# Two requests at a time on TensorE's column tiles for page scores and dilated values, and memory values with the weights as the stationary operand

## The chip, the cores and the metric

The kernel runs on one core of one Trainium2 chip. Its time is the device time of one launch in microseconds (us). Three runs of the kernel before gave 2172.45, 2179.99 and 2188.25 us, a median of 2179.99 us. A further run was recorded by the hardware profiler; every row below is from that one.

## The reference, cut to what matters

One decoder layer for two groups that share the weights: a prompt of 1024 tokens and 8 requests ("samples") of 4 new tokens each, with 1024 past keys. Everything is float32. Three small pieces of the samples' work matter here.

```python
# index scores of a request's 4 tokens against its 1024 past keys (pages of 128) and its new ones, 8 index heads
dots = einsum('bqhd,bsd->bqhs', qi, ki)                     # b = 8 requests, d = 64
score = einsum('bqh,bqhs->bqs', wi * IDX_SCALE, relu(dots)) # then the 256 best keys per token

# dilated windows, 3 groups with (window, dilation) = (128,1), (512,4), (2048,16), 4 heads of 64
kv_sel = kv_all[:, lb + t - dil * arange(m + 1)]            # per request
p = softmax(einsum('bqhd,bqkhd->bqhk', q, kv_sel[..., 0]) * scale)
o = einsum('bqhk,bqkhd->bqhd', p, kv_sel[..., 1])           # <- values, per request

# memory attention, 256 memory tokens per request, 4 heads of 64
p = softmax(einsum('bqhd,bkhd->bhqk', q, mem_kv[:, :, 0]) * scale)
o = einsum('bhqk,bkhd->bqhd', p, mem_kv[:, :, 1])           # <- values, per request
```

## The kernel before, in words

The program is a row of stages, each a block in which the five engines run their own instruction lists and meet by semaphores.

**Stage 1 (`project_and_select`, about 0 to 717 us)** projects all 1056 tokens with `w_in`, in 138 steps of 24 float32 products split in three (high and low halves of both operands). Steps 0 to 89 put tokens on the output's partitions (L955), steps 90 to 137 compute the gates (L961; nine steps for each 384 columns). Between two steps TensorE does pieces of other work, by a table of steps:

- `PAGES_AT`: steps 44, 46, ..., 60. At step 44 + 2b, `turn_pages(b)` transposes the index keys of request b (8 transposes, L1019) into `pt`; ScalarE's `take_pages(b)` copies them to `kis_t[:, b % 2]`; and `dot_pages(b - 1)` scores the request before (L1028: 64 rows of contraction, a stationary operand of 32 columns, two halves of 512 moving columns). Request b's 32 rows (4 tokens by 8 heads) are partitions `32 * (b % 4)` on of `big[:, b // 4]`.
- VectorE picks the best keys in rounds (`best`: MAX8 L859, MATCH_REPLACE8 L862). In its last 24 rounds it also sums one "window unit" a round (L893, `s_logit`).
- A window unit is one (group, request) of `WIN_UNITS`, 24 in all, group by group. SyncE loads queries and keys (`load_near`, from step 86 on; the query load of unit u waits for logit u - 3), GpSimd multiplies (`products`, L762 to L767), VectorE sums. At step 127 (`LOGITS_AT`) TensorE turns the logits (L1071), and SyncE starts loading values.
- `READ_AT`: after each of the steps 131 to 136, `read_values` of four units in turn. Group 0 has one matmul a unit, groups 1 and 2 have four (one for each residue t). All have a stationary operand of 32 columns (`spread[g]`, where the weights of a pair of requests stand side by side in zeros) and 256 moving columns of values (L1091), and add to 32 partitions of `big[:, 1, 0:256]`: `row = 32 * (b // 2)`. So the two requests of a pair share a row strip. The values of unit u are in `v_near[u % 4]`; the load of unit u waits for the read of unit u - 4 (`s_read`), at L444. A unit's values are 128 KB in group 0, 512 KB in group 1, 256 KB in group 2 (64 partitions).

**Stage 4 (paged attention of the samples)** is not changed, but it does similar work: `score_pair` (L2087) issues the matmuls of two requests one behind the other into different strips of 32 partitions, and its values (L2131) go over four strips in turn.

**Stage 6 (`attend_mem`, about 1295 to 1450 us)** does the memory attention. The samples' part lies inside the prompt's: in iteration `it` TensorE computes logits of prompt tile `it` (L2853), transposes the weights of tile `it - 1` (L2873, after ScalarE's four exponentials, L2615), and multiplies tile `it - 2` with the values (L2885). At `it == 0` it turns the samples' weights (L2801); at `it == 1` it runs `mem_values` (L2810): for each request, each half c of the 256 value columns and each half a of the memory tokens, one matmul with the values as the 128 x 128 stationary operand and the request's 16 columns of weights as the moving one. The result is already transposed, and ScalarE's `sample_rows` (L2599) and VectorE's `sample_low` (L2711) take it out of `p_o`. The values of prompt tile 0 at `it == 2` reuse `p_o`, so TensorE waits for `sample_low` (`s_slo`).

In the profile one float32 matmul appears as two MATMUL records. The line numbers are those of the profile.

Of the kernel before, what the change touches and what calls it, by code (L numbers as in the profile page):

```python
# [91 lines left out]
WIN_UNITS = [(g, b) for g in range(3) for b in range(DB)]  # L92
# [82 lines left out]
def project_and_select(nc, d, sel, spare):  # L175
# [6 lines left out]
    with ctx:  # L182
# [204 lines left out]
        with nc.Block() as block:  # L387
# [541 lines left out]
            def _(pe):  # L929
# [92 lines left out]
                def dot_pages(b):  # L1022
                    u, r = b // 4, 32 * (b % 4)
                    pe.wait_ge(s_kptev, b + 1)
                    if b == 0:
                        pe.wait_ge(s_relu, len(dots))
                    for e in range(2):
                        m = pe.matmul(big[r:r + 32, u, 512 * e:512 * e + 512], qis_t[:, u, r:r + 32], kis_t[:, b % 2, 512 * e:512 * e + 512],  # L1028
                                      start=True, stop=True)
                    m.then_inc(s_sdot, 1)  # L1030
# [50 lines left out]
                def read_values(u):  # L1081
                    g, b = WIN_UNITS[u]
                    w = WIN_KEYS[g]
                    row = 32 * (b // 2)
                    if u == 0:
                        pe.wait_ge(s_ptev, 1)
                        pe.matmul(big[:, 1, 0:256], probs_new, v_new, start=True, stop=False, skip_group_check=True)
                    pe.wait_ge(s_vnear[u % 4], 16 * (u // 4 + 1))
                    for t in range(WIN_RES[g]):
                        x = 32 * (b * WIN_RES[g] + t)  # L1090
                        m = pe.matmul(big[row:row + 32, 1, 0:256], spread[g][0:w, x:x + 32], v_near[u % 4][0:w, t * 256:(t + 1) * 256],  # L1091
                                      start=False, stop=True, skip_group_check=True)
                    m.then_inc(s_read, 1)

                for s in range(FIRST_STEP[NIDX], len(STEPS)):
# [7 lines left out]
                    if s in PAGES_AT:  # L1103
                        b = PAGES_AT[s]
                        if b < DB:
                            turn_pages(b)
                        if b:
                            dot_pages(b - 1)
# [12 lines left out]
                    for u in READ_AT.get(s, []):  # L1121
# [1320 lines left out]
def attend_mem(nc, d, km_t, vm, h_t, n, inv_in, inv_out, w_first, w_first_r, gains, kept):  # L2442
# [6 lines left out]
    with ctx:  # L2449
# [20 lines left out]
        probs_st = sb("probs_st7", [P, 2, P])  # L2470
# [30 lines left out]
        s_sptev = sem("f_sptev")  # L2501
        s_spv = sem("f_spv")
# [36 lines left out]
        with nc.Block() as block:  # L2539
# [20 lines left out]
            def _(act):  # L2560
# [29 lines left out]
                def sample_weights():  # L2590
                    act.wait_ge(s_spt, 1)
                    act.activation(probs_st[:, :, :], p_x[:, 0:256].rearrange("p (a c) -> p a c", a=2), ACT.Copy).then_inc(s_sptev, 1)
# [9 lines left out]
                for it in range(LAST):  # L2602
# [15 lines left out]
                    if it == 1:  # L2618
                        sample_weights()
                    if it == 2:  # L2620
# [26 lines left out]
            def _(pool):  # L2647
                pool.memset(q_bd[:, :, :], 0.0).then_inc(s_pad, 1)
# [1084 lines left out]
```

## Time and profile before

| | |
|---|---|
| median of three runs | 2179.99 us |
| the profiled run's own time | 2187.04 us |
| its span (first to last instruction) | 2185.3 us |
| TensorE matmul busy | 2027.0 us (93%) |
| VectorE, ScalarE, GpSimd busy | 1282.0, 718.0, 579.9 us |
| mean granted TensorE clock | 0.956 |

### The profile page before, as it was taken

Reading aid. Unit: us, or ns where it says so; the run is one execution under the profiler, and the core shown is the slowest. Engines: PE = TensorE matmul, PEld = TensorE weight load, DVE = VectorE, ACT = ScalarE, POOL = GpSimd, SP = SyncE. Lnnn points to the kernel's source line nnn. Section 1 sums busy time; section 2 is a strip of 40 time slices with the busy share of each in tenths; the row PEclk is TensorE's granted clock in tenths of the full one; section 3 lists DMA queues with packets and bytes.
Section 4 is the critical chain, followed back from the end, with each engine's and each line's share of the span. In section 5 each row is a group of like instructions: output and inputs, shape, how many; then the busy total and the mean of one; then the engine's idle time right before and its main releaser. Section 6 shows DMA issues by size and latency. Waiting matters only on the chain. (4 is left out here: it accounts for less than half of the span.)

```text
span 2185.3 us, 35149 instructions
## 1 busy us (share of the span) xinstructions
PE 2027.0 (93%) x13531; PEld 1850.8 (85%) x13531; DVE 1282.0 (59%) x2470; ACT 718.0 (33%) x1478; POOL 579.9 (27%) x671
## 2 busy tenths in 40 slices
PE   6999899999999786889779989999999999999997
PEld 6878788999996675555469989899999999999997
DVE  5049999998770342554337323677676676653535
ACT  5233222112220554334322124563233233332523
POOL 5786646678970001100100120120000000301000
PEclk9999999999999887799889998899999999999999
DMA  5022132346744613784336202012222222534434
GB/s 177 15 86 77 64 93 69 103 154 196 238 150 149 230 55 85 239 282 157 98 117 203 68 20 89 10 56 69 84 81 72 84 80 73 197 120 153 135 90 138
DMA packets 227162, 254.16 MB, mean 116 GB/s; under 512 B 51684, under 2 KB 209540, under 8 KB 226484
## 3 DMA queue, kind: packets, MB, share of 16 engines
q1 hardware_dynamic: 192292, 170.92, 25.9%
q0 software_dynamic: 8080, 51.13, 6.5%
q10 hardware_dynamic: 26624, 29.87, 3.9%
q8 instruction: 108, 1.77, 0.3%
q14 instruction: 58, 0.48, 0.1%
HBM read 205.18 MB, written 74.00 MB: 128 GB/s over the span
## 5 line engine op out<-in xcount | busy, mean ns | idle before, releaser
L955 PE MATMUL pz<-w_hi,n_hi 128*128 128x384 f32 (+2 forms) x720 | 246.5, 342 | 1.7 <-ACT z L537 1.0
L955 PE MATMUL pz<-w_hi,n_lo 128*128 128x384 f32 (+2 forms) x720 | 240.5, 334 | 0.0
L955 PE MATMUL pz<-w_lo,n_hi 128*128 128x384 f32 (+2 forms) x720 | 240.5, 334 | 0.0
L862 DVE MATCH_REPLACE8 sel<-m,sel 128x1024 f32<-128x1024 f32 (+4 forms) x224 | 205.4, 922 | 0.0
L859 DVE MAX8 m<-sel 128x8 f32<-128x1024 f32 (+4 forms) x224 | 197.6, 926 | 0.2
L3575 PE MATMUL p_c<-n_t_hi,blk 128*128 128x264 f32 x1120 | 191.3, 285 | 1.8 <-DVE blk L3292 1.8
L3575 PEld LDWEIGHTS p_c<-n_t_hi,blk 128*128 128x128 f32 x1120 | 159.0, 188 | 2.0 <-issue 2.0
L955 PEld LDWEIGHTS pz<-w_hi,n_hi 128*128 128x128 f32 x720 | 138.8, 193 | 24.5 <-issue 21.3
L3575 PE MATMUL p_c<-mix_hi,blk 128*128 128x264 f32 x816 | 141.1, 285 | 0.0
L955 PEld LDWEIGHTS pz<-w_lo,n_hi 128*128 128x128 f32 x720 | 138.9, 193 | 0.0
L955 PEld LDWEIGHTS pz<-w_hi,n_lo 128*128 128x128 f32 x720 | 138.8, 193 | 0.0
L961 PE MATMUL pz<-n_hi,w_hi 128*128 128x352 f32 x384 | 125.7, 327 | 3.5 <-ACT z L531 3.5
L537 ACT ACTIVATE z<-pz 128x384 f32<-128x384 f32 (+2 forms) x90 | 42.7, 475 | 251.7 <-PE pz L955 211.3
L961 PE MATMUL pz<-n_lo,w_hi 128*128 128x352 f32 x384 | 124.1, 323 | 0.0
L961 PE MATMUL pz<-n_hi,w_lo 128*128 128x352 f32 x384 | 124.1, 323 | 0.0
L3575 PEld LDWEIGHTS p_c<-mix_hi,blk 128*128 128x128 f32 x816 | 116.4, 189 | 0.0
L727 POOL TENSOR_TENSOR rot<-z,rope 128x384 f32<-128x384 f32 (+3 forms) x90 | 75.6, 840 | 152.9 <-ACT z L537 150.9
L709 POOL TENSOR_TENSOR w_lo<-w_raw,w_hi 128x1536 fp32r<-128x1536 f32 (+3 forms) x32 | 106.1, 3315 | 36.0 <-ACT w_hi L504 36.0
L3575 PE MATMUL p_c<-n_t_lo,blk 128*128 128x264 f32 x560 | 113.9, 284 | 0.0
L3175 POOL DMA_DIRECT2D g_s<-gate x22 | 12.0, 545 | 368.6 <-DVE gate L3380 343.5
L1302 DVE CUSTOM_DVE_ANT_0 probs<-p_s,masks 128x128 f32<-128x128 f32 (+1 forms) x96 | 28.1, 349 | 137.1 <-PE p_s L1367 130.8
L3616 PE MATMUL p_c<-n_t_hi,blk 128*128 128x264 f32 x540 | 105.0, 286 | 1.6 <-DVE blk L3406 0.9
(485 smaller groups left out, 5265.6 us busy)
## 6 DMA issues: line engine op xcount, KB each, us to landing
w_raw<-in_w_in SPq DMA_DIRECT2D x26, 768.0 KB, 4.8
blk_raw<-in_w_ffn_in SPq DMA_DIRECT2D x72, 256.0 KB, 2.9
relu<-z_qb SPq DMA_DIRECT2D x24, 512.0 KB, 4.8
blk_raw<-in_w_ffn_out SPq DMA_DIRECT2D x58, 192.0 KB, 2.5
z_b<-z ACTq DMA_DIRECT2D x48, 192.0 KB, 1.9
gates<-z ACTq DMA_DIRECT2D x48, 176.0 KB, 3.1
gate<-gates SPq DMA_DIRECT2D x24, 352.0 KB, 3.4
out_new_win_sample<-in_cache_win_kv POOLq DMA_DIRECT2D x8, 1016.0 KB
```

Source lines behind the costliest of these rows:

```text
L537: act.activation(z[:, u, 0:w], pz[:, s % 2, 0:w], ACT.Copy).then_inc(s_zev, 1)
L709: pool.tensor_tensor(w_lo[:, n % 2, 4 * j:4 * j + 4, 0:w], w_raw[:, f % RAW, :, 0:w], w_hi[:, n % 2, 4 * j:4 * j + 4, 0:w].bitcast(F32), A ...
L727: pool.tensor_tensor(a, z[:, u, 0:nh * HD].rearrange("p (h e) -> p h e", h=nh), cos, ALU.mult)
L859: dve.max(out=m8[0:r, u, :], in_=sel[0:r, o:o + n]).then_inc(s_max, 1)
L862: dve.match_replace(out=sel[0:r, o:o + n], in_to_replace=m8[0:r, u, :], in_values=sel[0:r, o:o + n], imm_value=PICKED).then_inc(s_rep, 1)
L955: m = pe.matmul(out, tokens(a, k, i), b[:, n % 2, k, 0:w], start=(k == 0 and p == 0), stop=(k == KC - 1 and p == 2))
L961: m = pe.matmul(out, a[:, n % 2, k, i * P:(i + 1) * P], b[:, k, third * THIRD:(third + 1) * THIRD], start=(k == 0 and p == 0), stop=(k == ...
L1302: t = dve.tensor_tensor_reduce(out=probs[:, u, h * w:(h + 1) * w], in0=p_s[:, j % 2, c:c + w], in1=masks[:, m0:m0 + w], scale=-ATT_SCALE, ...
L3175: pool.dma_start(d["g_s"][f * P:(f + 1) * P, half * HALF:(half + 1) * HALF], (gate, u3)[half][:, :, :].rearrange("p a c -> p (a c)")).then ...
L3575: m = pe.matmul(p_c[:, 2 * x + q, 0:QUART], a[:, w], b[:, q * QUART:(q + 1) * QUART], start=(k == 0 and y == 0), stop=(k == 3 and y == 2))
L3616: last = pe.matmul(p_c[:, out_bank(x), 0:QUART], a[:, cols], b[:, q * QUART:(q + 1) * QUART], start=(f == 0 and y == 0), stop=(f == FC - 1 ...
```

## The change

Three places, and nothing else:

1. `dot_pages(b0)` scores two requests at once, at every second page step, ahead of that step's `turn_pages`. The two requests' matmuls alternate and go to different strips of 32 partitions.
2. `WIN_UNITS` takes the requests in the order 0, 2, 4, 6, 1, 3, 5, 7 within each group, so that neighbouring units have different row strips, and `read_values(u0)` handles two units: it waits for the values of both and then alternates their matmuls.
3. `mem_values` takes the weights as the stationary operand (32 columns, from `probs_st` with each request's 16 columns set in zeros) and the 256 value columns as the moving one. The 16 matmuls go round four strips of `p_o[:, 256:512]`. The result has requests on partitions, so ScalarE copies it out (`sample_sum`) and TensorE transposes it (`turn_mem_rows`, at `it == 2`) before `sample_rows`. `probs_st` and the copied rows lie in `k_t`; GpSimd clears `probs_st` once the memory logits are done; ScalarE's `sample_weights` becomes two copies.

```diff
-WIN_UNITS = [(g, b) for g in range(3) for b in range(DB)]
+WIN_UNITS = [(g, b) for g in range(3) for b in (0, 2, 4, 6, 1, 3, 5, 7)]
...
-                def dot_pages(b):
-                    u, r = b // 4, 32 * (b % 4)
-                    pe.wait_ge(s_kptev, b + 1)
-                    if b == 0:
+                def dot_pages(b0):
+
+                    pe.wait_ge(s_kptev, b0 + 2)
+                    if b0 == 0:
                         pe.wait_ge(s_relu, len(dots))
                     for e in range(2):
-                        m = pe.matmul(big[r:r + 32, u, 512 * e:512 * e + 512], qis_t[:, u, r:r + 32], kis_t[:, b % 2, 512 * e:512 * e + 512],
-                                      start=True, stop=True)
-                    m.then_inc(s_sdot, 1)
+                        for b in (b0, b0 + 1):
+                            u, r = b // 4, 32 * (b % 4)
+                            m = pe.matmul(big[r:r + 32, u, 512 * e:512 * e + 512], qis_t[:, u, r:r + 32], kis_t[:, b % 2, 512 * e:512 * e + 512],
+                                          start=True, stop=True)
+                            if e:
+                                m.then_inc(s_sdot, 1)
...
+                    for u in (u0, u0 + 1):
+                        pe.wait_ge(s_vnear[u % 4], 16 * (u // 4 + 1))
                     for t in range(WIN_RES[g]):
-                        x = 32 * (b * WIN_RES[g] + t)
-                        m = pe.matmul(big[row:row + 32, 1, 0:256], spread[g][0:w, x:x + 32], v_near[u % 4][0:w, t * 256:(t + 1) * 256],
-                                      start=False, stop=True, skip_group_check=True)
-                    m.then_inc(s_read, 1)
+                        for u in (u0, u0 + 1):
+                            b = WIN_UNITS[u][1]
+                            row, x = 32 * (b // 2), 32 * (b * WIN_RES[g] + t)
+                            m = pe.matmul(big[row:row + 32, 1, 0:256], spread[g][0:w, x:x + 32], v_near[u % 4][0:w, t * 256:(t + 1) * 256],
+                                          start=False, stop=True, skip_group_check=True)
+                            if t == WIN_RES[g] - 1:
+                                m.then_inc(s_read, 1)
...
                         b = PAGES_AT[s]
+                        if b and b % 2 == 0:
+                            dot_pages(b - 2)
                         if b < DB:
                             turn_pages(b)
-                        if b:
-                            dot_pages(b - 1)
...
-                    for u in READ_AT.get(s, []):
+                    for u in READ_AT.get(s, [])[::2]:
                         read_values(u)
...
                     act.wait_ge(s_spt, 1)
-                    act.activation(probs_st[:, :, :], p_x[:, 0:256].rearrange("p (a c) -> p a c", a=2), ACT.Copy).then_inc(s_sptev, 1)
+                    act.wait_ge(s_clear, 1)
+                    for half in range(2):
+                        e = act.activation(probs_st[:, :, :].rearrange("p a (q x) -> p a q x", q=4)[:, :, :, 48 * half:48 * half + 16],
+                                           p_x[:, 0:256].rearrange("p (a q x) -> p a q x", a=2, q=4)[:, :, :, 16 * half:16 * half + 16], ACT.Copy)
+                    e.then_inc(s_sptev, 1)
+
+                def sample_sum():
+                    act.wait_ge(s_rows, 1)
+                    act.activation(mem_rows, p_o[:, 256:512], ACT.Copy).then_inc(s_rowsev, 1)
...
                     if it == 1:
                         sample_weights()
+                        sample_sum()
...
+                pool.wait_ge(s_g, DB)
+                pool.memset(probs_st[:, :, :], 0.0).then_inc(s_clear, 1)
...
-                    for b in range(DB):
-                        for c in range(2):
-                            for a in range(2):
-                                x = pe.matmul(p_o[:, c * P + 16 * b:c * P + 16 * b + 16], v_s[:, b, a, c * P:(c + 1) * P],
-                                              probs_st[:, a, 16 * b:16 * b + 16], start=(a == 0), stop=(a == 1))
+                    for odd in range(2):
+                        for a in range(2):
+                            for q in range(4):
+                                b = 2 * q + odd
+                                x = pe.matmul(p_o[32 * q:32 * q + 32, 256:512], probs_st[:, a, 32 * b:32 * b + 32], v_s[:, b, a, :],
+                                              start=(odd == 0 and a == 0), stop=(odd == 1 and a == 1))
+                    x.then_inc(s_rows, 1)
+
+                def turn_mem_rows():
+                    pe.wait_ge(s_rowsev, 1)
+                    for c in range(2):
+                        x = pe.transpose(p_o[:, c * P:(c + 1) * P], mem_rows[:, c * P:(c + 1) * P], ident[:, :])
                     x.then_inc(s_spv, 1)
...
+                    if it == 2:
+                        turn_mem_rows()
```

## Rows read from the trace of the kernel before

**Rows 1.** Busy time by stretch: PE, PEld, DVE, ACT, POOL; clock, DMA share, GB/s.
```profile
262.00:372.00 110.00, 110.00 (x586) 94.44 (x585) 109.69 (x161) 26.28 (x39) 64.57 (x88) 1.00 0.27 83
```
**Rows 2.** Timeline of TensorE, page steps 44 and 46: start, us, instruction.
```profile
268.15 1.03 PE L1019 MATMUL pt<-ident,gain 128*64 128x128 f32 x8
...
268.95 0.42 PE L955 MATMUL pz<-w_hi,n_hi 128*128 128x384 f32 x1
...
277.50 1.04 PE L1019 MATMUL pt<-ident,gain 128*64 128x128 f32 x8
278.47 1.90 PE L1028 MATMUL big<-x_in,qis_t 64*32 64x512 f32 x4
...
280.30 0.44 PE L955 MATMUL pz<-w_hi,n_hi 128*128 128x384 f32 x1
```
**Rows 3.** Timeline of TensorE, stage 4, a pair of requests scored.
```profile
1073.06 1.91 PE L2087 MATMUL p_s<-k_t,q_t 128*32 128x512 f32 x8
```
**Rows 4.** Timelines of SyncE's queue and TensorE; waits of 500 to 716 us (total, times, longest).
```profile
499.43 0.33 SPq L416 DMA_DIRECT2D relu<-z_qb  x1
...
643.57 0.64 PE L1071 MATMUL pt<-ident,qi_t 128*128 128x128 f32 x3 [0.96 <-DVE qi_t L893]
...
DVE qi_t L893 <- POOL relu L767: 26.9, 8, 6.6
```
**Rows 5.** Timeline of TensorE, reads after step 131 (units 0 to 3).
```profile
660.65 0.40 PE L1091 MATMUL big<-qi_t,relu 128*32 128x256 f32 x1
660.66 0.40 PE L1091 MATMUL big<-x_in,relu 128*32 128x256 f32 x1
...
661.65 0.43 PE L961 MATMUL pz<-n_hi,w_hi 128*128 128x352 f32 x1
```
**Rows 6.** Timeline of TensorE, reads after steps 133 and 134 (units 8 to 15).
```profile
671.45 1.91 PE L1091 MATMUL big<-qi_t,relu 128*32 128x256 f32 x8 [0.67 <-DMA qi_t<-in_cache_win_kv]
674.48 1.91 PE L1091 MATMUL big<-qi_t,relu 128*32 128x256 f32 x8 [1.12 <-DMA qi_t<-in_cache_win_kv]
676.07 3.64 PE L1091 MATMUL big<-x_in,relu 128*32 128x256 f32 x16
...
683.71 2.99 PE L1091 MATMUL big<-qi_t,relu 128*32 128x256 f32 x13
686.33 0.40 PE L1091 MATMUL big<-x_in,relu 128*32 128x256 f32 x1
...
689.90 0.43 PE L961 MATMUL pz<-n_hi,w_hi 128*128 128x352 f32 x1
```
**Rows 7.** DMA issues of 655 to 716 us: size, median us from issue to landing.
```profile
qi_t<-in_cache_win_kv SPq DMA_DIRECT2D x4, 512.0 KB, 5.4
...
qi_t<-in_cache_win_kv SPq DMA_DIRECT2D x4, 256.0 KB, 3.6
```
**Rows 8.** A longer wait in stage 1: timeline of TensorE, and busy time after it.
```profile
256.52 1.65 PE L1002 MATMUL big<-ki_t,qi_t 64*128 64x384 f32 x4 [4.41 <-ACT relu L608]
...
258.00:261.00 3.00, 3.00 (x11) 2.90 (x10) 2.90 (x5) 0.36 (x1) 0.00 (x0) 0.50 0.68 255
```
**Rows 9.** Timelines of TensorE and ScalarE around the memory values; busy time in them.
```profile
1355.48 1.09 PE L2873 MATMUL p_t<-ident,probs 128*128 128x128 f32 x8 [1.98 <-ACT probs L2615]
1356.41 13.44 PE L2810 MATMUL p_o<-probs_st,v_s 128*128 128x16 f32 x64
...
1374.17 1.97 PE L2885 MATMUL p_o<-inv_ffn,probs_t 128*128 128x64 f32 x16 [0.42 <-DVE om_lo L2711]
...
1356.61 0.60 ACT L2608 ACTIVATE probs_t<-p_t 128x512 f32<-128x512 f32 x1 [0.91 <-PE p_t L2873]
...
1369.88 0.80 ACT L2599 ACTIVATE om_hi<-p_o 64x32 fp32r<-64x32 f32 x4 [10.86 <-PE p_o L2810]
...
1358.00:1370.00 12.00, 12.00 (x58) 11.96 (x60) 0.00 (x0) 1.14 (x7) 0.00 (x0) 0.50 0.00 1
```
**Rows 10.** Busy time in stage 4's values (L2131), four strips in turn.
```profile
1112.00:1116.00 4.00, 3.77 (x72) 3.35 (x72) 0.00 (x0) 0.17 (x1) 0.00 (x0) 0.50 0.02 4
```

More of the change, by code:

```diff
@@ L1079, in turn_probs, with read_values @@
                     t.then_inc(s_pt, 1)
-                def read_values(u):
-                    g, b = WIN_UNITS[u]
+                def read_values(u0):
+                    g = WIN_UNITS[u0][0]
                     w = WIN_KEYS[g]
-                    row = 32 * (b // 2)
-                    if u == 0:
+                    if u0 == 0:
                         pe.wait_ge(s_ptev, 1)
                         pe.matmul(big[:, 1, 0:256], probs_new, v_new, start=True, stop=False, skip_group_check=True)
-                    pe.wait_ge(s_vnear[u % 4], 16 * (u // 4 + 1))
+                    for u in (u0, u0 + 1):
+                        pe.wait_ge(s_vnear[u % 4], 16 * (u // 4 + 1))
                     for t in range(WIN_RES[g]):
-                        x = 32 * (b * WIN_RES[g] + t)
-                        m = pe.matmul(big[row:row + 32, 1, 0:256], spread[g][0:w, x:x + 32], v_near[u % 4][0:w, t * 256:(t + 1) * 256],
-                                      start=False, stop=True, skip_group_check=True)
-                    m.then_inc(s_read, 1)
+                        for u in (u0, u0 + 1):
[5 more added lines that the diff above has]
+                                m.then_inc(s_read, 1)
                 for s in range(FIRST_STEP[NIDX], len(STEPS)):
@@ L2469, in attend_mem @@
         probs_s = sb("probs_s7", [P, 256])
-        probs_st = sb("probs_st7", [P, 2, P])
+        probs_st = k_t[:, 0, :].rearrange("p (a c) -> p a c", a=2)
+        mem_rows = k_t[:, 1, 0:256]
         st = sb("st7", [P, 4])
@@ L2501, in attend_mem @@
         s_sptev = sem("f_sptev")
+        s_clear = sem("f_clear")
+        s_rows = sem("f_rows")
+        s_rowsev = sem("f_rowsev")
         s_spv = sem("f_spv")
```

## The prediction

> **What bounds the kernel now.** I read the page's busy shares first: TensorE is busy 93% of the span. A mean share proves nothing about one stage, so I then asked of each of the three edited places whether TensorE sets its pace. (1) In the stretch of the page scores TensorE is busy 110.00 of 110 us [rows 1]. VectorE is as full, but with its own rounds of picking; its unit sums come later and wait for GpSimd 26.9 us in 8 waits [rows 4], and GpSimd's products follow TensorE's steps. So a shorter step there moves everything behind it. (2) In the reads of the dilated values TensorE is busy too, except for two waits for values that a DMA brings, 0.67 and 1.12 us [rows 6]. This is where a faster engine will meet the transfers. (3) In the memory values TensorE runs the 64 records without a gap, at a granted clock of 0.50, which is 1.2 of 2.4 GHz [rows 9]; nothing else of the stage goes on.
>
> **Do strips run side by side?** All gains hang on this. Two requests in different strips, 8 records of 512 columns, last 1.91 us [rows 3]; one request, 4 such records, lasts 1.90 us, and the next work starts 1.83 us after it [rows 2]. So two strips cost what one does. In the first reads, units 0 and 2 start 0.01 us apart [rows 5]. With four strips, 72 records of 128 columns fit into 4 us at clock 0.50 [rows 10], 0.053 us each; one strip alone would need about 0.215 us a record (an estimate: 256 columns take 0.215 us at full clock, see part 2, so half the columns take as long at half of it), four times as much. So four strips overlap in full.
>
> **Part 1, page scores.** Before: eight times 1.83 us [rows 2]. After: four pairs at 1.84 us, the same with the 0.01 us more of [rows 3]. Those pairs contract over 128 rows and these over 64; the single request with 64 rows lasts as long as the pair with 128, so I take the same price. 14.6 - 7.4 = 7.3 us (7.28 unrounded). Besides, the eight transposes take 0.97 us when scores follow and 0.80 us when a projection follows [rows 2]: one change of tile shape less, at four steps, 0.7 us if all of it goes. The wait for the second request's copy ended two steps before. `turn_pages` now stands behind the scores, 1.84 us later in its step; its copy has the next step to hide in. Together 7.3 to 8.0 us; I take 7.6.
>
> Does it reach the end of stage 1? TensorE meets the chain again at step 127, where it waits 0.96 us for VectorE's last sum [rows 4]. That sum is late because GpSimd was, and GpSimd follows ScalarE's weight halves, hence TensorE. What does not move is VectorE's own picking: the fourth query load is issued at 499.43 us [rows 4], when VectorE has its first sum, at its own pace. GpSimd would like that load up to 8 us earlier. VectorE catches up after it (the 26.9 us are slack), so I expect the delay to be absorbed. If half of it were not, part 1 would give 3.8; if none, 0.
>
> **Part 2, dilated values.** One unit of group 1 or 2 is 8 records. Sixteen records that follow one another in a strip last 3.64 us and 8 last 1.91 [rows 6]: 8 more for 1.73 us, so 0.215 us a record of 256 columns at full clock. After each step the reads take 1.00 us (131, 132), 8.2 us (133, waits inside), and 6.19 us (134; 135 and 136 the same to 0.01) [rows 5, 6]: 28.8 us.
>
> Here a rule of the Trainium skill bears. What the row shows: at step 134 the first record of unit 14 starts at 686.33 [rows 6], while unit 13, ahead of it in program order, is still issuing (13 + 3 records of 0.215 us from 683.71 end at 687.15). The Trainium skill, TensorE: Matmul & The Clock Gate (Part 3, The mechanism), says that matmuls start strictly in program order. By that rule the reads before would hold no overlap, 32 records in 6.9 us, and halving would give 3.4 a step. The row shows 6.19, so some of the gain is already had.
>
> With two strips busy throughout, four units take 16 x 0.215 = 3.4 us: 2.8 us less in each of the steps 134 to 136, some 0.4 us in 131 and 132 each, and at 133 all that is not the wait. Without transfers the sum would be 2 x 0.4 + 4.8 + 3 x 2.8 = 14 us. But the transfers bind:
>
> - Step 133: TensorE arrives at 670.8 - 0.8 = 670.0. Now it needs units 8 *and* 9; unit 9 lands at 674.5, its load issued 0.4 us earlier, so 674.1. Before, unit 8 was read meanwhile; now TensorE stands 4 us.
> - After a wait of 4.41 us the clock was 0.50 for the next 3 us of work [rows 8]. So I price the first pair at half clock, 3.4 us, to 677.5, and the second at between 1.7 and 3.4, to about 679.9 (before: 679.7). Nothing gained at 133.
> - Step 134: units 12 and 13 are loaded once 8 and 9 are read, which is now at 677.5 for both instead of 673.4 and 676.4. At 5.4 us from issue to landing [rows 7] they are there at about 683, TensorE at 684.1. Units 14 and 15, issued at 680, two at a time, land at 686.5: wait 0.7, then 1.7. The step ends at 688.3 against 689.90, a gain of 1.6.
> - Steps 135 and 136: loads of half the size, 3.6 us [rows 7], issued over 4 us ahead. Both steps gain 2.7 on top, less 0.3 for unit 19's tail.
>
> Part 2 gives 1.6 + 2 x 2.7 - 0.3 = 6.7 us. If the clock holds in step 133, 8. If transfers follow more slowly or the clock stays low a step longer, 3. I take 6.7 with 3 and 10 as ends.
>
> **Part 3, memory values.** Before, from 1356.41 to the first values of the prompt at 1374.17: 17.8 us [rows 9]. After: 32 records of 256 columns over four strips, 8 rounds. A round is 0.215 us at full clock and 0.43 at half. The clock had fallen before 1358, behind TensorE's 1.98 us wait [rows 9], and nothing of that is changed: 3.4 us, to 1359.9. Then a chain that was not there: ScalarE had copied and done its exponentials while TensorE was in the memory values; now it waits in `sample_sum` for them, and behind that wait are queued the copy of transposed weights and the four exponentials of tile 1. Copy of the rows 0.4 (between the 0.6 of 512 columns and half of it), copy of weights 0.6, exponentials 2.0 (TensorE waited 1.98 for tile 0's) [rows 9]: 1362.9. TensorE has logits of tile 2 and the two new transposes to do meanwhile (eight records and two; by the 0.93 that eight transposes take at full clock, from 1355.48 to the next start, an estimate of 2.3 at half clock), then the transposes of tile 1, 0.93 at full clock or 1.9 at half [rows 9], to 1365.0 at the latest. `sample_rows` (0.80 [rows 9]) and `sample_low` (taken as long) follow the exponentials and end at 1364.5. So the prompt's values start between 1364.5 and 1365.0 instead of 1374.17, which gives 9.2 to 9.7 us; I take 9.3. With the clock held throughout, 1.7 + 0.4 + 0.6 + 2.0 + 0.8 + 0.8 end at 1362.7, a gain of 11.4, the high end. The second copy in `sample_weights` hides under TensorE's transposes of tile 0 (0.93 us); GpSimd does nothing else in this stretch, so its clearing is done long before. Low end: had the clock not fallen in the old code, its 64 records would take half, and the gain would be 3; the low clock through the whole 12 us says that such matmuls do not raise it, so I give that little weight.
>
> **Sum.** 7.6 + 6.7 + 9.3 = 23.6 us of the profiled run's 2187.04: 2163.4. The median of the runs shown lies 7.0 below it; moved by the same 23.6, it becomes 2156.4 us, 1.08% less. About 1%, 21.8 us, is what a measurement of this kernel tells from no change.
>
> **Rivals.** (a) *As forecast*, all three parts reach the end. (b) *The picking holds the first part*: GpSimd's products start when VectorE lets them, TensorE's wait at step 127 grows from 0.96 to some 8 us, and 16 us are left: 2164. For it: the fixed load at 499.43; against: 26.9 us of slack. (c) *The transfers never bind and the clock holds*: 7.6 + 12 + 11.4 = 31: 2149. Against: the waits that were there already. (d) *The clock*: new waits in step 133 and in the memory part leave TensorE at 1.2 GHz for more work behind them. To end slower it must cost more than 23.6 us, so 47 us of TensorE's work at half clock (it loses half of it). The wait of 4.41 us in dense work was followed by some 3 us at 0.50 [rows 8], so this is a long way. At 65 us of such work it gives 2156.4 + 32.5 = 2189. (e) *The strips do not overlap when neighbours alternate*: then parts 1 and 2 give 0, or lose a changeover of 0.17 us by [rows 2] at each of their 104 alternating matmuls (32 and 72), 18 us, plus the 4 us wait of step 133; part 3, four times slower in its matmuls, gives nothing: about 2202. Against it are [rows 3, 10].
>
> **Chances.** (a) 0.60; (b) 0.17; (c) 0.17; (d) 0.03; (e) 0.03. Around (a) the parts' ends and the spread of the runs (2172 to 2188, a median good to some 4 us) put a third of it within 1%, so faster is 0.45 of (a) and all of (c), 0.62; same is the rest of (a), (b) and (d), 0.35; slower is (e), 0.03. The range takes in (b) and most of (c): 2147 to 2168.
>
> **What would show it.** Page steps: one L1028 row of 8 records and about 1.8 us, four times. L1071's wait still about 1 us (b: 8). Reads: a wait of about 4 us before the first of step 133, then records at half clock; 3.4 us a step in 135 and 136. Memory: L2810's records in under 4 us, a wait of TensorE before L2873. Wrong if L1071 waits several us more, if reads still take 6 us, or if waits downstream grow.

## The result and the profile after

The changed kernel takes 2157.09 us (median of four runs, 2154.87 to 2160.99) against 2181.13 us of the kernel before: a ratio of 0.9893, with a 95% interval from 0.9862 to 0.9923. That is 24 us less by the medians, and 1.07% by the ratio; 23.6 us and 2156.4 us were forecast. The total was right. Of its three terms the one for the page scores was some 3 us too high, the one for the memory values 1 to 3 us too low, and these errors cancelled.

The profiled run has a span of 2153.5 us, 31.8 us under that of before. I go through the three places in the order of time. The change shifted the lines of the kernel: the page scores are L1030 (was L1028), the transposes of the logits L1074 (was L1071), the value reads L1096 (was L1091), the memory values L2832 (was L2810).

**Page scores.** Timeline of TensorE in the changed kernel, steps 46 and 48 (start, us, instruction); it answers to [rows 2].

```profile
276.09 1.03 PE L1019 MATMUL pt<-ident,gain 128*64 128x128 f32 x8
276.88 0.42 PE L955 MATMUL pz<-w_hi,n_hi 128*128 128x384 f32 x1
...
285.48 1.91 PE L1030 MATMUL big<-x_in,qis_t 64*32 64x512 f32 x8
287.32 1.06 PE L1019 MATMUL pt<-ident,gain 128*64 128x128 f32 x8
288.14 0.42 PE L955 MATMUL pz<-w_hi,n_hi 128*128 128x384 f32 x1
```

Eight records of two requests take 1.84 us from start to next start, as four records of one did. The transposes take 0.79 us where no scores are beside them and 0.82 where they stand behind scores; before, they took 0.97 us at each of the seven steps where scores followed them.

**The gate steps.** Waits from step 90 to step 127 in the changed kernel (total us, times, longest); they answer to [rows 4].

```profile
POOL relu L762 <- DMA x_in<-in_cache_win_kv: 8.1, 2, 6.6
...
PE pz L961 <- ACT z L531: 5.6, 4, 3.1
```

The row of GpSimd's wait for keys (`POOL relu L762`) is new. Its reason is in the timelines of GpSimd, SyncE's queue, VectorE and TensorE there.

```profile
498.41 0.75 POOL L767 TENSOR_TENSOR relu<-relu 128x256 f32<-128x256 f32 x1
505.71 2.42 POOL L762 TENSOR_TENSOR relu<-x_in,relu 128x1024 f32<-128x1024 f32 x1 [6.56 <-DMA x_in<-in_cache_win_kv]
...
510.29 3.46 POOL L709 TENSOR_TENSOR w_lo<-w_raw,w_hi 128x1536 fp32r<-128x1536 f32 x1
...
501.72 0.33 SPq L416 DMA_DIRECT2D relu<-z_qb  x1
502.09 0.43 SPq L420 DMA_DIRECT2D x_in<-in_cache_win_kv  x1
...
501.30 0.40 DVE L893 TENSOR_REDUCE qi_t<-relu 128x16 f32<-128x256 f32 x1
...
513.85 0.40 PE L961 MATMUL pz<-n_hi,w_hi 128*128 128x352 f32 x1 [1.93 <-issue]
...
637.28 0.58 PE L1074 MATMUL pt<-ident,qi_t 128*128 128x128 f32 x3
```

To be read backwards: TensorE stands 1.93 us at step 99, because the low half of the next weights is late (GpSimd writes it from 510.29 to 513.75); GpSimd computes it behind the product of unit 3; that product waited 6.56 us for its keys; their load is issued at 502.09, queued in SyncE behind the query load at 501.72; and that one had to wait for VectorE's first sum, at 501.30. The transposes of the logits start at 637.28, 6.3 us earlier than before and without a wait (0.96 us before).

VectorE's first sum did not only keep its time, it came 2.3 us later than before (499.01). Most of the delay arises in one pair of instructions. Timelines of VectorE before, then of VectorE and GpSimd in the changed kernel:

```profile
348.12 2.28 DVE L868 TENSOR_SCALAR sel<-sel 128x1024 f32<-128x1024 f32 x2
...
347.16 5.28 DVE L868 TENSOR_SCALAR sel<-sel 128x1024 f32<-128x1024 f32 x2
...
347.08 3.46 POOL L709 TENSOR_TENSOR w_lo<-w_raw,w_hi 128x1536 fp32r<-128x1536 f32 x1
```

The two instructions at L868 take 3.0 us longer. GpSimd, which got ahead with TensorE, now splits the next weights while they run. In all eleven kernels below with the paired page scores one of these two instructions lies beside this split and takes 3.9 or 4.0 us; in the three without them neither takes more than 1.44 us. Counted from the start of stretch A (see below), the first sum comes 3.1 to 3.8 us later in the eight of the eleven that leave VectorE's order alone. No run moves the split away, so that the split is the cause is read from this coincidence and not tested.

**Value reads.** Timeline of TensorE and granted clock (PEclk, third number from the end of a stretch) at steps 133 to 136; they answer to [rows 5, 6].

```profile
666.40 3.27 PE L1096 MATMUL big<-qi_t,relu 128*32 128x256 f32 x16 [2.83 <-DMA qi_t<-in_cache_win_kv]
669.57 1.92 PE L1096 MATMUL big<-x_in,relu 128*32 128x256 f32 x16
671.42 0.43 PE L961 MATMUL pz<-n_hi,w_hi 128*128 128x352 f32 x1
...
675.91 1.92 PE L1096 MATMUL big<-qi_t,relu 128*32 128x256 f32 x16 [0.34 <-DMA qi_t<-in_cache_win_kv]
679.15 1.92 PE L1096 MATMUL big<-x_in,relu 128*32 128x256 f32 x16 [1.32 <-DMA x_in<-in_cache_win_kv]
681.00 0.43 PE L961 MATMUL pz<-n_hi,w_hi 128*128 128x352 f32 x1
...
692.10 1.92 PE L1096 MATMUL big<-qi_t,relu 64*32 64x256 f32 x16
694.38 1.92 PE L1096 MATMUL big<-x_in,relu 64*32 64x256 f32 x16 [0.36 <-DMA x_in<-in_cache_win_kv]
```

```profile
667.00:669.00 2.00, 2.00 (x14) 0.93 (x11) 0.00 (x0) 0.00 (x0) 0.00 (x0) 0.50 0.89 319
```

A pair's 16 records last 1.92 us where one unit's 8 lasted 1.91. At step 133 there is a wait where one of 4 us was forecast (2.83 us) and behind it the forecast half clock (3.27 us for a pair), and step 134 waits twice for loads, 1.66 us.

**Memory values.** Timeline of TensorE and the granted clock; they answer to [rows 9].

```profile
1336.42 1.09 PE L2903 MATMUL p_t<-ident,probs 128*128 128x128 f32 x8 [1.98 <-ACT probs L2633]
1337.45 1.93 PE L2832 MATMUL p_o<-v_s,k_t 128*32 128x256 f32 x32
1339.31 1.14 PE L2881 MATMUL p_s<-inv_ffn,qm_t 64*128 64x256 f32 x8
1340.38 0.44 PE L2839 MATMUL p_o<-ident,k_t 128*128 128x128 f32 x2
1342.20 1.09 PE L2903 MATMUL p_t<-ident,probs 128*128 128x128 f32 x8 [1.38 <-ACT probs L2633]
```

```profile
1336.00:1342.00 6.00, 4.39 (x50) 2.68 (x50) 2.09 (x3) 3.26 (x14) 0.00 (x0) 1.00 0.00 0
```

The 32 records take 1.86 us. ScalarE is now the one that TensorE waits for (1.38 us, the exponentials of tile 1 behind `sample_sum`). The clock did not fall here, behind the same wait of 1.98 us as before; the forecast's main sum had it at half.

### The profile page after: what moved, and what is told of

Its sections match the earlier page's. It is cut to its first block and busy times, and to the rows that moved or that the text cites. A ratio compares the mean times of both kernels' runs of the same rounds, so it can differ in the third digit from the quotient of the medians.

```text
span 2153.5 us, 35105 instructions
## 1 busy us (share of the span) xinstructions
PE 1983.7 (92%) x13501; PEld 1821.6 (85%) x13501; DVE 1284.4 (60%) x2470; ACT 719.1 (33%) x1480; POOL 582.2 (27%) x672
## 3 DMA queue, kind: packets, MB, share of 16 engines
q0 software_dynamic: 8080, 51.13, 6.6%
## 5 line engine op out<-in xcount | busy, mean ns | idle before, releaser
L709 POOL TENSOR_TENSOR w_lo<-w_raw,w_hi 128x1536 fp32r<-128x1536 f32 (+3 forms) x32 | 106.0, 3312 | 30.4 <-ACT w_hi L504 30.4
```

What stands on the lines that cost most here:

```text
L709: pool.tensor_tensor(w_lo[:, n % 2, 4 * j:4 * j + 4, 0:w], w_raw[:, f % RAW, :, 0:w], w_hi[:, n % 2, 4 * j:4 * j + 4, 0:w].bitcast(F32), A ...
```

## The experiments

Each was profiled; the ones with a ratio were also timed beside the kernel before. Single runs of this program spread by 1%, so most questions are settled on four stretches of the profiled runs, all in us between starts on TensorE. A: from the transposes of the index queries (L1009) to the scores of the new keys. B: from there to the transposes of the logits. C: from the first value read to the stage's last transposes. D: from the first memory value to the output projection. A hardly scatters; kernels that run the same code in one of the others still differ there by some us (B by up to 3, C by up to 2, D by up to 5), so a difference of 1 or 2 us between two profiles is no evidence there.

| kernel | A | B | C | D |
|---|---|---|---|---|
| before | 99.65 | 280.20 | 54.62 | 49.61 |
| changed | 91.39 | 283.59 | 47.01 | 37.90 |
| e1 page scores alone | 91.38 | 283.66 | 53.88 | 54.59 |
| e2 value reads alone | 99.64 | 281.40 | 48.69 | 53.92 |
| e3 memory values alone | 99.48 | 278.57 | 53.57 | 40.14 |
| e4 changed, early sums | 91.38 | 279.18 | 47.47 | 40.47 |
| e5 changed, split first | 91.38 | 280.84 | 45.88 | 39.73 |
| e6 changed, mixed sizes | 91.44 | 279.81 | 47.03 | 37.90 |
| e7 changed, strip by strip | 91.38 | 283.81 | 46.28 | 41.75 |
| e8 changed, e4 and e6 | 91.34 | 274.13 | 49.34 | 38.45 |
| e9 changed once more | 91.38 | 285.64 | 48.13 | 38.71 |
| e10 changed, no alternation | 91.39 | 283.73 | 48.73 | 40.46 |
| e11 changed, old memory values | 91.38 | 282.59 | 47.08 | 49.32 |
| e12 e4, four units at once | 91.39 | 277.89 | 51.13 | 39.48 |

**e1, e2, e3: one part alone.** Each is the kernel before with the lines of one numbered point of the change, and no other edit.

> The kernel before with the paired page scores alone. My theory: four pairs at 1.84 us, so the matmul of the new keys starts 8.3 us earlier than before (363.4 less 8.3, give or take the start), but GpSimd then stands before the product of unit 3 (its keys are queued in SyncE behind a query load that needs VectorE's first sum at about 500 us), its low half of the weights comes late, and TensorE waits about 2 us at step 99; of the 8.3 us some 5 arrive at step 127. Time 2181 - 5 = 2176. Rival A: no loss on the way, all 8 arrive, 2173. Rival B: the loss in the gate steps is crowding of transfers and comes from the new order of the requests; then this kernel shows no wait at step 99 and all 8 us arrive. The memory values stay near 13.4 us if the clock falls as before, near 6.5 if it holds.

> The kernel before with the new order of the requests and the paired value reads alone. My theory: reads of 0.57, 0.57, then a wait of about 3 us and 5 us, then 5, 3 and 4.1 us; from the first read to the transposes at the stage's end 7.6 us less than before (54.6), nothing changed at step 99 and step 127. Time 2181 - 7.6 = 2173.5. Rival: the order of the requests moves loads in the gate steps, and part of the gain is lost before the reads; then step 127 comes later than 643 us. If transfers did not bind, the reads would be 14 us shorter: 2167.

> The kernel before with the new memory values alone. My theory: the memory values take 1.9 us at full clock (3.4 at half) and the prompt's first values start 6.3 us (8 at half clock) after them, so 9.5 to 11.4 us less: 2181 - 10.5 = 2170.5. Rival: the gain was the clock's, not the operands': then the clock's fall comes back here in other places behind the wait of 2 us, and the gain is 3 to 6 us.

Measured: ratios 0.9981 (0.9947 to 1.0015), 0.9973 (0.9941 to 1.0004) and 0.9953 (0.9923 to 0.9983), with medians of 2174.07, 2175.95 and 2169.87 us against 2177.7. Only the third is clear of 1. By the ratios the three are 4.1, 5.9 and 10.2 us, 20 of the 24, by the medians 3.6, 1.8 and 7.8; each interval reaches some 7 us either way, so the times alone do not show that they add up. The stretches say where. In e1, A falls by 8.27 and B rises by 3.5: some 5 of the 8 us arrive, as I had expected after seeing the profile. Its wait at step 99 was 0.42 us, not 2, though GpSimd waited for its keys here too (5.5 us); TensorE's waits for ScalarE's z there were 5.2 us against 3.5 before. With the 0.42 that is 2.1 of the 3.5 us; where the rest went is not shown. Rival B, that the loss belongs to the new order of requests, falls: e1 keeps the old order. In e2 the reads give 5.9 us (C: 54.62 to 48.69), not 7.6. There the wait before step 133 was 4.44 us, and both pairs behind it ran slowly:

```profile
675.94 3.63 PE L1093 MATMUL big<-qi_t,relu 128*32 128x256 f32 x16 [4.44 <-DMA qi_t<-in_cache_win_kv]
679.11 2.87 PE L1093 MATMUL big<-x_in,relu 128*32 128x256 f32 x16
```

```profile
674.00:681.00 7.00, 5.06 (x26) 2.54 (x28) 0.00 (x0) 0.00 (x0) 0.00 (x0) 0.52 0.47 156
```

It is tempting to say that the size of the wait decides whether the clock costs no pair, one or two. The other runs forbid it. In e5 TensorE waited 2.91 and 1.51 us at step 133, and both pairs ran at full clock; in e11 it waited 2.40 and 0.90 us, and the clock was at half for both.

```profile
663.98 1.92 PE L1098 MATMUL big<-qi_t,relu 128*32 128x256 f32 x16 [2.91 <-DMA qi_t<-in_cache_win_kv]
667.41 1.92 PE L1098 MATMUL big<-x_in,relu 128*32 128x256 f32 x16 [1.51 <-DMA x_in<-in_cache_win_kv]
...
666.33 2.86 PE L1096 MATMUL big<-qi_t,relu 128*32 128x256 f32 x16 [2.40 <-DMA qi_t<-in_cache_win_kv]
670.09 3.63 PE L1096 MATMUL big<-x_in,relu 128*32 128x256 f32 x16 [0.90 <-DMA x_in<-in_cache_win_kv]
```

The first two rows are e5's, the last two e11's. What decides it stays open. In e3 the memory values took 3.51 us, at half clock for most of it, and the gain in D was still 9.5 us against before.

**e4: VectorE's first sum earlier.** This undoes the hold of the page scores' gain.

```diff
-                for rnd in range(ROUNDS - len(WIN_UNITS)):
+                rnd = 0
+                for _ in range(ROUNDS - len(WIN_UNITS) - 4):
                     best(("s", 3, 2), rnd)
+                    rnd += 1
                 for u, (g, b) in enumerate(WIN_UNITS):
-                    best(("s", 3, 2), ROUNDS - len(WIN_UNITS) + u)
+                    best(("s", 3, 2), rnd)
+                    rnd += 1
+                    if u in (5, 9, 13, 17):
+                        best(("s", 3, 2), rnd)
+                        rnd += 1
```

> The changed kernel, with four of VectorE's plain rounds of picking moved from ahead of the first window sum to behind the sums of units 5, 9, 13 and 17, so that the first sum comes some 18 us earlier. If VectorE's own pace held the loads, GpSimd's wait before unit 3's product (6.6 us) and TensorE's at step 99 (1.9 us) go, and step 127 comes 4 us earlier than 637.3: 2157 - 4 = 2153. Rival: the gate steps are held by the stores of gates and the loads beside them; then TensorE's waits for ScalarE's z (5.7 us there) grow by what the other wait loses, and step 127 stays at 637: 2157.

Measured: B is 279.18, 4.4 us less than in the changed kernel and 1.0 less than before the change. The logits' transposes start at 634.72 where 633 was expected. The wait at step 99 is gone, and GpSimd's longest wait for keys is 2.7 us instead of 6.6. The waits for z did not grow:

```profile
POOL relu L762 <- DMA x_in<-in_cache_win_kv: 2.7, 1, 2.7
...
PE pz L967 <- ACT z L531: 3.6, 4, 1.3
```

So VectorE's pace was what held the gain: with its first sum at 488.26 instead of 501.30, all of A's 8.3 us arrive. The ratio to before is 0.9868 (0.9815 to 0.9921), the lowest of all, but the interval contains the changed kernel's 0.9893.

**e5: the needed half of the weights ahead of the waiting product.** It removes the queueing and leaves the late sum.

```diff
-                        for _ in range(2):
+                        for i in range(2):
+                            if n == len(PROJ) + 1 and j == 1 and i == 1:
+                                split_lo(n, j)
                             if u < len(WIN_UNITS):
                                 products(u)
                                 u += 1
...
-                        if n < len(COLS):
+                        if n < len(COLS) and (n, j) != (len(PROJ) + 1, 1):
                             split_lo(n, j)
```

> The changed kernel with one thing moved on GpSimd: the low half of the weights that TensorE needs at step 99 is computed before the product of unit 3, not behind it. The first sum on VectorE is as late as in the changed kernel. If the only loss were the split queued behind the product, TensorE's wait at step 99 (1.93 us) goes and the transposes of the logits come 2 to 4 us earlier than 637.3. Rival: the late loads crowd together behind the first sum anyway; then the wait at step 99 goes and the waits for ScalarE's z at steps 103 to 112 (5.6 us) take its place, and the time from the new keys' scores to the logits stays at 283.6 us (280.2 before the change, 279.2 with early sums).

Measured: B is 280.84, 2.75 us less, and the logits' transposes start at 634.72, 2.6 us earlier. The wait at step 99 is gone and the waits for z stay at 5.3 us (5.6 in the changed kernel). So the queueing behind one stalled product was over half of what e4 gave back (2.75 of 4.4 us); that the rest is the lateness itself is argued, not shown. It is one run, but the five other kernels with unmoved split and sums and this order (changed, e7, e9, e10, e11) lie between 282.6 and 285.6.

**e6: units of mixed sizes.**

```diff
-WIN_UNITS = [(g, b) for g in range(3) for b in (0, 2, 4, 6, 1, 3, 5, 7)]
+WIN_UNITS = [(0, b) for b in (0, 2, 4, 6, 1, 3, 5, 7)] + [(g, b) for pair in ((0, 2), (4, 6), (1, 3), (5, 7)) for g in (2, 1) for b in pair]
```

> The changed kernel with another order of the window units behind group 0: a pair of group 2 (256 KB a unit), then a pair of group 1 (512 KB), and so on. The bytes and matmuls are the same. If the transfers set the pace of the reads, each step now fetches 1.5 MB, the small ones first: a wait of 1 to 2 us before step 133's reads and perhaps 1 to 2 inside it, little or none later, and from the first read to the stage's last transposes 44 to 45 us (47.0 in the changed kernel). Rival: a wait is set by the issue and landing of single loads, not by bytes; then the sum stays at 47. Time 2157 - 2 = 2155 or 2157.

Measured: C is 47.03, unchanged; my hope was wrong. The waits before and in step 133 shrank to 1.47 and 0.98 us, but a later step's 32 records now take 3.70 us without a wait where the changed kernel's step 135 takes 2.95. That the different tile heights of its four units cause this is not shown: with equal heights, step 134 takes 3.57 us without a wait in e11 and 3.87 in e9. A gain came where I had not looked: B is 279.81, 3.8 us less, although TensorE still waited 1.96 us at step 99. The keys of the units come in the same mixed order, and TensorE's waits for z there fell from 5.6 us to 1.2; why is not shown. The ratio is 0.9887 (0.9839 to 0.9935).

**e7: the memory values strip by strip.**

```diff
-                    for odd in range(2):
-                        for a in range(2):
-                            for q in range(4):
+                    for q in range(4):
+                        for odd in range(2):
+                            for a in range(2):
                                 b = 2 * q + odd
```

> The changed kernel, with the 16 matmuls of the memory values ordered strip by strip (four in a row into one strip) instead of going round. Same operands. If overlap of strips in time is what makes them cheap, 32 records of 0.215 us at full clock with at most a few overlapping at each change of strip give 5 to 6.9 us instead of 1.86. Rival: the weights as stationary operand are the gain, and strips matter little: then 2 to 3 us.

```profile
1335.03 4.59 PE L2832 MATMUL p_o<-v_s,k_t 128*32 128x256 f32 x32
1339.56 1.13 PE L2881 MATMUL p_s<-inv_ffn,qm_t 64*128 64x256 f32 x8
```

4.53 us, between both expectations: of the 32 records' 6.9 us (at 0.215) 2.35 overlap, at three changes of strip, so 3.6 records a change. So the 13.4 us of before fall apart into three: at full clock the old 64 records would take some 7.2 us (an estimate from 0.112 us each, as e2's first ones went before the clock fell; at half clock each took 0.213), the weights as stationary operand bring that to 4.53, and going round the strips to 1.86.

**e10: pairs waited for together, but not alternated.**

```diff
-                    for t in range(WIN_RES[g]):
-                        for u in (u0, u0 + 1):
+                    for u in (u0, u0 + 1):
+                        for t in range(WIN_RES[g]):
```

> The changed kernel, with pairs waited for together as in it, but the four matmuls of the first unit issued before the four of the second. If two strips overlap only as far as TensorE looks ahead (4 records or so of 8), the reads of the steps without waits take about 5.5 to 6.2 us, as before the change, instead of 2.9. Rival: the new order of the requests is enough, since the neighbours are in different strips: then about 3.4 us.

```profile
684.61 2.16 PE L1096 MATMUL big<-qi_t,relu 64*32 64x256 f32 x13
686.39 0.40 PE L1096 MATMUL big<-x_in,relu 64*32 64x256 f32 x1
...
689.13 0.43 PE L961 MATMUL pz<-n_hi,w_hi 128*128 128x352 f32 x1
```

32 records take 4.52 us (4.53 and 4.53 in the two other steps without a wait), the same as in e7: the same pattern of eight records a strip. Neither expectation was right: three changes of strip give three overlaps of 3.6 records, where the kernel before had one a step (6.88 - 6.19 = 0.69 us, 3.2 records). C is 48.73: the new order of the requests and the pairwise wait alone bring 5.3 of the 6.8 us, and the alternation, which makes a step up to 1.6 us shorter, adds about 1.5 over all of them, which is within C's scatter.

**e8: e4 and e6 together; e9: the changed kernel again; e11: the old memory values.** e8 has both diffs above. e11 is the changed kernel with point 3 of the change taken back.

> The changed kernel with the early sums and the mixed order of the units together. From step 90 to the transposes of the logits 156 us (160.4 in the changed kernel), from the first read to the stage's last transposes 44 to 45 if the mixed order still has the gain that I hoped for, 47 as it measured. So 4 to 6 us less than the changed kernel beside it. Rival: both only remove the same crowding of transfers in the gate steps (early sums 156.0, mixed order alone 156.6), so together they give no more than one of them: 4 us.

> The changed kernel once more, on this chip and beside the others: 23.6 us under the kernel before, as forecast and as measured (24.0). Its profile tells whether the granted clock at the memory values is luck: a spell at 0.50 of 0 or 3.4 us, where the old ones had 17 to 24, if the new matmuls are what ends it.

> The changed kernel with the memory values of before (parts 1 and 2 alone). My theory now: the low clock of the memory values outlasts them, so the old ones cost more than the 9.3 us that I had priced: from the first memory value to the output projection 50 to 55 us instead of 38 to 40, and this kernel is 10 to 15 us slower than the changed one beside it. Rival, as forecast: 9.3 us slower.

Measured on one chip: 0.9883 (0.9852 to 0.9914) for e8, 0.9882 (0.9856 to 0.9908) for e9, 0.9930 (0.9903 to 0.9957) for e11; medians 2152.88, 2155.59 and 2164.54 against 2179.72. e9 repeats the result: 24.1 us. e11 is 0.48%, or 10.5 us, above e9 by the ratios, and 9.0 by the medians; that does not tell the 9.3 us of the rival from the 10 to 15 expected. Its memory values ran as before (timeline of TensorE in e11):

```profile
1328.92 13.29 PE L2816 MATMUL p_o<-probs_st,v_s 128*128 128x16 f32 x64
1342.14 2.08 PE L2859 MATMUL p_s<-inv_ffn,qm_t 64*128 64x256 f32 x8
```

Its granted clock over them (third number from the end):

```profile
1330.00:1346.00 16.00, 16.00 (x74) 14.86 (x73) 1.67 (x4) 2.30 (x12) 0.00 (x0) 0.50 0.00 1
```

D is 49.3 to 54.6 in the four kernels with old memory values (before, e1, e2, e11; mean 51.9), and 37.9 to 40.5 in the nine with the new ones in their order (mean 39.2). The difference of the means is 12.6 us, but the four fall in two groups: 49.6 and 49.3 in before and e11, where the clock was back when the prompt's first values began, and 54.6 and 53.9 in e1 and e2, where it was not. In e1 the stretch at 0.50 reached well past the memory values:

```profile
1337.00:1360.00 23.00, 22.58 (x102) 20.41 (x103) 4.71 (x12) 4.69 (x20) 0.00 (x0) 0.50 0.00 1
```

So my theory for e11, that the low clock outlasts the old memory values and costs more behind them, holds in two of four profiles, and e11 itself is not one of them.

e8's B of 274.13 is 9.5 us less than in the changed kernel, at least as much as e4 and e6 alone give together (4.4 and 3.8), so they are not one and the same crowding; but C is 49.34, with a wait of 1.52 us in step 136 and half clock behind it. The median is 2.7 us under e9's, and the ratios are equal: a gain that the timing did not resolve.

**e12: four units of group 2 at once** (on top of e4; `read_values` takes the number of units, 4 at steps 135 and 136).

```diff
+                    group = 4 if READ_AT.get(s, [0])[0] >= 16 else 2
-                    for u in READ_AT.get(s, [])[::2]:
-                        read_values(u)
+                    for u in READ_AT.get(s, [])[::group]:
+                        read_values(u, group)
```

> The kernel with early sums, with the four units of group 2 read in one round over four strips instead of two pairs, at steps 135 and 136. If strips overlap in full, 32 records take 1.9 us (8 rounds of 0.215 and the start) instead of 2.9 with two pairs. The loads then set the pace: all four must have landed, a wait of up to 1 us at step 136. Sum of reads 1 us less at step 135, 0 to 1 at 136. Rival: four strips of 256 columns are held by something else (the moving operands of four units), then 2.9 stays.

```profile
682.81 0.41 PE L1102 MATMUL big<-qi_t,relu 64*32 64x256 f32 x2 [0.86 <-DMA x_in<-in_cache_win_kv]
...
684.67 0.43 PE L967 MATMUL pz<-n_hi,w_hi 128*128 128x352 f32 x1
...
692.25 0.64 PE L1102 MATMUL big<-qi_t,relu 64*32 64x256 f32 x2 [3.43 <-DMA x_in<-in_cache_win_kv]
```

Four strips do overlap in full: 1.86 us for 32 records. But buffers come free together and late, and at step 136 TensorE waits 3.43 us and then runs the step at half clock, 3.57 us. C is 51.13, 3.7 us more than in e4. In this one run the faster read made the stretch slower.

## Why the prediction was right, and where it was not

**Strips side by side**: right for two strips and for four, at the price taken: 1.91 and 1.92 us for two; 1.86 us for 32 records in four.

**Part 1 (7.6 us forecast)**: the local gain was right, 8.2 us (A: 99.6 to 91.4). The changes of tile shape gave 1.0 of it, more than the forecast's 0.7 at most, because they went at seven steps and not at four. "I expect the delay to be absorbed" is the step that failed. The hold by VectorE, rival (b), is real: B is 283.8 on average (282.6 to 285.6) in the six kernels that have the page scores and no remedy (changed, e1, e7, e9, e10, e11), 280.1 (278.6 to 281.4) in the three without (before, e2, e3). The loss is 3.8 us and 4.4 arrive. I had looked at VectorE's slack, which is large in sum (26.9 us), and not at who is queued behind the one late load: SyncE, then GpSimd, then the split of the weights, then TensorE. e4 and e5 show that order. I had also taken VectorE's own picking for fixed, and its first sum came 2.3 us later. Rival (b) was wrong in size (all 7.6 lost) and in place: TensorE waits at step 99 and for ScalarE's z, and not at all at step 127.

**Part 2 (6.7 us)**: right in size. C falls from 54.0 (before, e1, e3) to 47.2 on average (changed, e2, e4, e5, e7, e9, e11), 6.8 us. By steps, from start to start of the projections, the changed kernel's profile has 1.8 us at 131 to 133, 0.7 at 134, 3.2 at 135 and 2.0 at 136; the forecast's own times make that -0.2, 1.8, 2.7 and 2.4. The wait at 133 was 2.8 instead of 4.0 us, because the load landed 12.2 us after the first read and not 13.5, and the second pair there ran at full clock; step 134 had 1.66 us of waits instead of 0.7. The argument that transfers and the clock decide this part was right: 6.8 us came of the 14 that the forecast estimates without them. Whether the clock falls is luck here, as e5 (C: 45.88, no fall) and e2 (48.69, two pairs at half) show.

**Program order.** In e10 the first record of unit 18 starts at 686.39 (the second row there), when three records of unit 17, ahead of it in the program and in another strip, have yet to start; e7's times fit the same at its three changes of strip. The Trainium skill, TensorE: Matmul & The Clock Gate (Part 3, The mechanism), says that matmuls start strictly in program order. Across strips these traces do not agree with it.

**Part 3 (9.3 us)**: mechanism right, size a little off. Within the stretch that I priced, first memory value to the prompt's first values, 17.8 us became 6.3 in the changed kernel, a gain of 11.4, and 7.9 in e3, a gain of 9.9; forecast were 9.2 to 9.7, and 11.4 with the clock held. The forecast's main sum had the clock at half for the new matmuls. It was so in e3, and it was not in the changed kernel: the wait of 1.98 us ahead of them is the same in both, so this was luck. What I left out lies behind the stretch: in e1 and e2 the old matmuls left the clock at 0.50 for 7.4 and 8.7 us after the prompt's first values began, which costs half of that, 3.7 and 4.4 us. In before and e11 the clock was back by then, and it cost nothing. "That such matmuls do not raise it" was seen; that the low clock could outlast them was not.

**The sum** by the stretches of the two profiles that the forecast is about: part 1 gives 8.3 - 3.4 = 4.9 us, part 2 gives 7.6, part 3 gives 11.7, together 24.2, against 7.6, 6.7 and 9.3 forecast. By the means over all kernels it is 4.4 + 6.8 + 12.6 = 23.8 us. That the total met the forecast to half a microsecond is luck: some 3 us too much in one term, and as much too little in the other two. By timing, part 3 is 10.2 us (e3) or 10.5 (e11), so how much of the 2 us above that is real is open.

**A slip in rival (e).** Its 104 alternating matmuls add 32 records of the page scores to 72 matmuls of the reads. The 32 records are 16 matmuls, so its changeovers come to 88 times 0.17, 15 us and not 18. Nothing hangs on it: the strips overlap.

**The profiled span** fell by 31.8 us, more than the medians. Of this, 24.2 are A to D in this pair of traces, and 4.9 lie between the end of stage 1 and the memory values, in code that is the same. That stretch took from 626.1 us (e1) to 642.5 us (e4) over all kernels here, and where it is long its mean granted clock tends to be low:

```profile
709.00:1335.00 626.00, 531.66 (x3254) 434.97 (x3255) 266.13 (x783) 237.70 (x577) 55.05 (x83) 0.92 0.46 143
```

```profile
699.00:1341.00 642.00, 546.32 (x3255) 447.98 (x3256) 265.46 (x783) 238.30 (x577) 55.60 (x84) 0.89 0.45 140
```

The first is e1, the second e4. This is why no single run settles a few microseconds here.

## What to carry to other kernels

Work on few columns is cheap when neighbours in program order go to different strips of the array; wide stationary operands with few moving columns are dear twice, by themselves and because in all four kernels that had them TensorE's clock was at half through nearly all of them, and in two of the four for 10 us or more of the work behind. When one engine gets ahead, don't count the others' slack in sum: look for the first thing that keeps its own time, and list what is queued behind it on every queue (here a load, a product, a split, a projection); moving one small item in front of the stalled one gave back over half. An engine that gets ahead also meets other work than before: here GpSimd's split came to lie beside a VectorE instruction that then took 3.9 us instead of 0.9 (L868). And a read that frees its buffers together can lose more in the next transfers than it saves.

## What was not expected of the hardware

- TensorE takes up 3 to 4 records of another strip beside the last records of the strip before (4.53 us for 32 records in four blocks of eight, 6.19 in two of sixteen, 1.86 all round).
- Two alternating pairs of group 2, one behind the other, can take less than the 3.4 us of two strips: 2.95 us for the 32 records of step 135 in the changed kernel. The same step takes from 2.75 (e4) to 3.53 us (e11) in other kernels, and why is open.
- Around one and the same wait of 1.98 us the clock stayed at 1.00 over the memory values in the changed kernel, e6, e7 and e9, and fell to 0.50 between 2.3 us before their start and 1.5 us behind it in the ten others. What decides it was not tried.
- A VectorE instruction of 0.7 to 1.4 us (L868) took 3.9 or 4.0 us in each of the eleven kernels where GpSimd's split of the weights (L709) ran beside it. VectorE's first sum came 3.1 to 3.8 us later with it, about as much as was lost of part 1's gain. What the two share was not tried.
